# Four blocks of two transformer layers in split fp32: both activation buffers start at another byte of 128

## The chip, the cores and the metric

The kernel runs on one core of a Trainium2 chip. The metric is the time of one execution in microseconds of the device, as the median of several runs. Engines in the profile: PE is TensorE's matmuls, PEld its weight loads, DVE VectorE, ACT ScalarE, POOL GpSimd, SP the engine that issues most transfers.

## What is computed

A sequence of 256 tokens of width 1024 goes through two models of two layers each. Each layer has two FFNs with SwiGLU and hidden width 2816, and between them a mixer: two banded attentions and a stick-breaking one in the first model, with cross-attention to a memory of 256 rows, and differential attention beside an mLSTM in the second. All of it is fp32. The greater part of the arithmetic is matrix products of this kind:

```python
def swiglu(h, w_gu, w_down):
    g, u = jnp.split(h @ w_gu, 2, axis=-1)
    return (jax.nn.silu(g) * u) @ w_down
...
x = x + FFN_SCALE * rmsnorm(swiglu(h, ffn1_w_gu[l], ffn1_w_down[l]), ffn1_norm_post[l])
h = rmsnorm(x, mix_norm_pre[l])
z = h @ w_in[l]
```

## The kernel before

Activations lie transposed: the 1024 features are 8 chunks (`C`) of 128 partitions, the 256 tokens (`T`) the free dimension. The weights come as a stream of 829 tiles of 128 x 1024 fp32 (512 KB), in the order in which they are used. SP loads tile n into one of four slots of `raw`. ScalarE rounds it to the type float32r into `w_hi` (line 1037), VectorE writes the rest `raw - w_hi`, rounded too, into `w_lo` (line 1471); both are rings of six slots. An activation is split in the same way into a high and a low part. A product is then three matmuls in float32r: high weight by high activation, high weight by low activation, low weight by high activation. TensorE issues nearly all of its matmuls through one helper, `mm`, at line 457.

The split activations live in two buffers, `a` and `b`, of shape 128 x 8 x 2 x 256: for each chunk the 256 columns of the high part and behind them the 256 of the low part. There are four forms in which TensorE reads them:

- `w_tile`, `three` and `tail_part`: per chunk three matmuls, each with 128 x 128 of weights stationary and 256 columns of `a` or `b` moving; 24 matmuls for one weight tile.
- `pair_tile` and `first_three`: as high and low part lie side by side, `w_hi` takes both in one matmul of 512 columns (`both`), and `w_lo` the high part in one of 256; eight chunks, 16 matmuls. This is used for gate and up of the FFNs.
- `down` in `ffn`: the hidden values of one step are in a chunk of the other buffer, and 24 matmuls of 256 columns add the product to the accumulators.
- `v_half`: the values of attention, with the roles exchanged: 128 columns of `a` or `b` stationary and 256 columns of a weight tile moving.

`a` is written by the norm ahead of each stage (`high` at line 1057 on ScalarE, `low` at line 1498 on VectorE), `b` by the hidden values in the FFN (lines 1092 and 1471) and by the outputs of attention. After a cross-attention the two exchange their roles, which is why both appear in both in the profile. TensorE takes the tiles in the order of the stream and waits per tile for the splits, and per chunk for the norm when the activation is fresh.

The order of the allocations is `raw`, a gap of 16 bytes, `a`, `b`, a gap of 48 bytes, `x`, `z` and the other buffers, a gap of 48 bytes, `w_hi`, `w_lo`, constants. Each allocation takes a multiple of 32 bytes. In the program's table of addresses, per partition, `raw` starts at byte 16512, `a` at 32928, `b` at 49312, `x` at 65760, `z` at 73952 and `w_hi` at 163168. Modulo 128 that is 0 for `raw`, 32 for `a` and `b`, and 96 for `x`, `z`, `w_hi` and `w_lo`. All pieces of `a`, `b` and the weight tiles that a matmul takes begin at multiples of 512 bytes from the start of their buffer, so these remainders are the remainders of every matmul's operands.

Of the kernel before, what the change touches and what calls it, by code (L numbers as in the profile page):

```python
# [24 lines left out]
F32R = mybir.dt.float32r  # L25
# [4 lines left out]
P = 128  # L30
D = 1024
T = 256
C = D // P
# [108 lines left out]
def build(nc, stream_d, x_d, mem_d, vec_d, con_d, biasa_d, biasc_d, heads_d, out_d, stages=STAGES):  # L142
    total = sum(TILES[s] for s, _ in stages)
    with ExitStack() as ctx:
        def sb(name, shape, dt=F32):
            return ctx.enter_context(nc.sbuf_tensor(name, shape, dt))
# [3 lines left out]

        raw = sb("raw", [P, RAW, D])
        sb("gap_a", [P, 4])
        a_two, b_two = sb("a", [P, C, 2, T], F32R), sb("b", [P, C, 2, T], F32R)
        a_hi, a_lo = a_two[:, :, 0, :], a_two[:, :, 1, :]
        b_hi, b_lo = b_two[:, :, 0, :], b_two[:, :, 1, :]
        sb("gap_x", [P, 12])
# [2121 lines left out]
```

## Time and profile before

| | us |
|---|---|
| median of 3 runs | 2693.83 (2691.82 to 2696.59) |
| the profiled execution | 2694.12 |
| its span in the trace | 2692.0 |
| PE busy | 2613.1 (97%) |
| PEld busy | 2410.1 (90%) |
| DVE busy | 1920.5 (71%) |
| ACT busy | 1502.9 (56%) |

A row of a group has the line, engine and operation, then output <- inputs by the buffers' names, for a matmul the moving operand first and the stationary one second, then shapes and count; behind the bar the busy time of the group, the mean of one instruction in ns, the idle time of the engine just before them and who ended it. A matmul's duration is modelled and holds its way through the array, so that durations of successive ones overlap; how often TensorE starts one is read from the starts in the timeline. The timeline merges neighbours of the same kind (x2). "Clock" (PEclk) is the share of TensorE's full clock that was granted.

### The profile page before, as it was taken

Reading aid. Unit: us, or ns where it says so; the run is one execution under the profiler, and the core shown is the slowest. Engines: PE = TensorE matmul, PEld = TensorE weight load, DVE = VectorE, ACT = ScalarE, POOL = GpSimd, SP = SyncE. Lnnn points to the kernel's source line nnn. Section 1 sums busy time; section 2 is a strip of 40 time slices with the busy share of each in tenths; the row PEclk is TensorE's granted clock in tenths of the full one; section 3 lists DMA queues with packets and bytes.
Section 4 is the critical chain, followed back from the end, with each engine's and each line's share of the span. In section 5 each row is a group of like instructions: output and inputs, shape, how many; then the busy total and the mean of one; then the engine's idle time right before and its main releaser. Section 6 shows DMA issues by size and latency. Waiting matters only on the chain.

```text
span 2692.0 us, 51716 instructions
## 1 busy us (share of the span) xinstructions
PE 2613.1 (97%) x18604; PEld 2410.1 (90%) x18604; DVE 1920.5 (71%) x3131; ACT 1502.9 (56%) x2579; POOL 201.6 (7%) x280
## 2 busy tenths in 40 slices
PE   8999799999999999999999999999999999999998
PEld 7998699999998899999998998989989999988997
DVE  7777676778777576777777667777787776676876
ACT  6556556556555656556555555655565555555554
POOL 0001001000000201000000160000000005300000
PEclk9999899999999999999999999999999999999999
DMA  7554244655554344555654543545545545335553
GB/s 261 202 189 135 87 134 156 225 202 183 186 187 157 102 158 136 188 186 169 204 187 142 179 157 103 165 154 185 186 154 187 187 143 171 126 118 165 172 187 109
DMA packets 122821, 445.80 MB, mean 166 GB/s; under 512 B 13688, under 2 KB 14712, under 8 KB 122688
## 3 DMA queue, kind: packets, MB, share of 16 engines
q1 hardware_dynamic: 120816, 436.79, 49.0%
q0 software_dynamic: 1872, 7.17, 0.7%
q8 instruction: 92, 1.51, 0.2%
q14 instruction: 41, 0.34, 0.0%
HBM read 442.86 MB, written 1.05 MB: 165 GB/s over the span
## 4 chain that ended last, share of the span: by engine, by line
PE 92%; DVE 5%; ACT 2%; issue 1%; DMA 0%; SPq 0%; ACTq 0%; DVEq 0%
PE bank L457 91%; DVE w_lo L1471 1%; PE bank L808 1%; DVE rt L1699 1%; DVE z L1537 1%; ACT w_hi L1037 0%; DVE rt L1493 0%; DVE x L1530 0%; DVE a L1498 0%; ACT score L1271 0%; DMA x<-in_x_dram 0%; DVE rstd_x L1490 0%; DMA raw<-in_stream_dram 0%; ACT L1245 0%; DVE z L1643 0%
## 5 line engine op out<-in xcount | busy, mean ns | idle before, releaser
L457 PE MATMUL bank<-a,w_hi 128*128 128x256 f32 (+1 forms) x5360 | 1342.3, 329 | 38.5 <-DVE a L1498 38.0
L1471 DVE TENSOR_TENSOR w_lo<-raw,w_hi 128x1024 fp32r<-128x1024 f32 x829 | 1016.7, 1230 | 278.3 <-ACT w_hi L1037 277.1
L457 PE MATMUL bank<-a,w_lo 128*128 128x256 f32 x3736 | 1013.2, 282 | 0.0
L457 PEld LDWEIGHTS bank<-a,w_hi 128*128 128x128 f32 x5360 | 897.4, 190 | 126.2 <-issue 45.7
L1037 ACT CAST w_hi<-raw 128x1024 fp32r<-128x1024 f32 x829 | 858.0, 1046 | 42.6 <-DMA raw<-in_stream_dram 35.4
L457 PE MATMUL bank<-b,w_hi 128*128 128x256 f32 (+1 forms) x4096 | 859.5, 301 | 3.6 <-DVE b L1498 2.6
L457 PEld LDWEIGHTS bank<-a,w_lo 128*128 128x128 f32 x3736 | 709.2, 190 | 16.8
L457 PEld LDWEIGHTS bank<-b,w_hi 128*128 128x128 f32 x4096 | 656.9, 188 | 40.6 <-issue 3.5
L457 PE MATMUL bank<-b,w_lo 128*128 128x256 f32 x2400 | 658.6, 280 | 0.0
L457 PEld LDWEIGHTS bank<-b,w_lo 128*128 128x128 f32 x2400 | 450.4, 188 | 5.6
L1084 ACT COPY pt<-bank 128x256 f32<-128x256 f32 x176 | 65.5, 372 | 219.1 <-PE bank L457 219.1
L1080 ACT COPY pt<-bank 128x256 f32<-128x256 f32 x176 | 65.3, 371 | 219.2 <-PE bank L457 219.2
L2033 POOL TENSOR_TENSOR score<-score 128x256 f32<-128x256 f32 x45 | 38.2, 848 | 1367.6 <-ACT score L1067 1366.6
L1550 DVE TENSOR_TENSOR sil<-bank,pt 128x256 f32<-128x256 f32 x176 | 74.6, 424 | 88.6 <-ACT pt L1080 88.6
L1092 ACT CAST b<-hmid 128x256 fp32r<-128x256 f32 x132 | 53.7, 407 | 142.6 <-PE bank L457 133.1
L457 PE MATMUL bank<-w_hi,a 128*128 128x256 f32 x736 | 129.6, 280 | 0.0
L457 PEld LDWEIGHTS bank<-w_hi,a 128*128 128x128 f32 x736 | 111.7, 188 | 3.4 <-issue 2.9
L1643 DVE TENSOR_TENSOR z<-bank,rstd_x 128x256 f32<-128x256 f32 x125 | 52.8, 422 | 83.3 <-PE bank L457 83.1
L1556 DVE TENSOR_TENSOR hmid<-bank,pt 128x256 f32<-128x256 f32 x176 | 74.5, 424 | 44.2 <-ACT pt L1084 44.1
L457 PE MATMUL bank<-w_lo,a 128*128 128x256 f32 x368 | 102.3, 278 | 0.0
L1471 DVE TENSOR_TENSOR b<-hmid,b 128x256 fp32r<-128x256 f32 x132 | 56.0, 424 | 45.7 <-ACT b L1092 45.7
L1088 ACT ACTIVATE sil<-sil 128x256 f32<-128x256 f32 x176 | 74.3, 422 | 21.3 <-DVE sil L1561 21.2
(185 smaller groups left out, 2130.7 us busy)
## 6 DMA issues: line engine op xcount, KB each, us to landing
raw<-in_stream_dram SPq DMA_DIRECT2D x829, 512.0 KB, 3.3
z<-in_biasc_dram POOLq DMA_DIRECT2D x6, 512.0 KB, 4.5
z<-in_biasa_dram POOLq DMA_DIRECT2D x3, 512.0 KB, 4.4
x<-in_x_dram SPq DMA_DIRECT2D x2, 512.0 KB, 8.0
v<-in_mem_dram POOLq DMA_DIRECT2D x2, 512.0 KB, 6.3
out_dram<-x SPq DMA_DIRECT2D x8, 128.0 KB, 1.9
con<-in_con_dram POOLq DMA_DIRECT2D x1, 912.0 KB, 6.6
vec<-in_vec_dram POOLq DMA_DIRECT2D x1, 417.0 KB, 5.6
```

Source lines behind the costliest of these rows:

```text
L457: return nc.tensor.matmul(out, lhsT, rhs, start=start, stop=stop, skip_group_check=shared)
L808: last = nc.tensor.transpose(out[:, col:col + P], p[:, src:src + P], ident)
L1037: nc.scalar.copy(w_hi[:, slot, :], raw[:, raw_slot, :]).then_inc(hi_split, 1)
L1080: nc.scalar.copy(pt[:, j % 2, 0:T], bank[ffn_banks(j, after_mixer)[0]][:, T:2 * T]).then_inc(gate_rest, 1)
L1084: nc.scalar.copy(pt[:, j % 2, T:2 * T], bank[ffn_banks(j, after_mixer)[1]][:, T:2 * T]).then_inc(up_rest, 1)
L1088: nc.scalar.activation(sil[:, jj, :], sil[:, jj, :], ACT.Silu).then_inc(silu_done, 1)
L1092: nc.scalar.copy(high_of["b"][:, jj, :], hmid[:, jj, :]).then_inc(hhi_done, 1)
L1471: return nc.vector.tensor_tensor(out, a, hi.bitcast(F32), ALU.subtract)
L1550: nc.vector.tensor_tensor(sil[:, jj, :], bank[ffn_banks(j, after_mixer)[0]][:, 0:T], pt[:, jj, 0:T], ALU.add)\
L1556: nc.vector.tensor_tensor(hmid[:, jj, :], bank[ffn_banks(j, after_mixer)[1]][:, 0:T], pt[:, jj, T:2 * T], ALU.add).then_inc(up_read, 1)
L1643: nc.vector.tensor_tensor(z[:, tile, :], out[:, 0:T], rstd[norm][:, :], ALU.mult).then_inc(w_evac, 1)
L2033: ins = nc.gpsimd.tensor_tensor(sq[:, 0, :], sq[:, 0, :], sq[:, c, :], ALU.add)
```

## The change

Both buffers get a room that is 32 words (128 bytes) longer than their content. The content of `a` begins 2 words (8 bytes) into its room, that of `b` 30 words (120 bytes) into its own. Modulo 128, `a` goes from 32 to 40 and `b` from 32 to 24. Everything allocated behind them moves up by 256 bytes and keeps its remainder modulo 128; `raw` stays. The views `a_hi`, `a_lo`, `b_hi`, `b_lo` are taken as before, and no instruction, order or wait is touched.

```diff
-        a_two, b_two = sb("a", [P, C, 2, T], F32R), sb("b", [P, C, 2, T], F32R)
+        ROOM, A_AT, B_AT = 32, 2, 30
+        a_room, b_room = sb("a", [P, C * 2 * T + ROOM], F32R), sb("b", [P, C * 2 * T + ROOM], F32R)
+        a_two, b_two = (room[:, at:at + C * 2 * T].rearrange("p (c s t) -> p c s t", s=2, t=T)
+                        for room, at in ((a_room, A_AT), (b_room, B_AT)))
         a_hi, a_lo = a_two[:, :, 0, :], a_two[:, :, 1, :]
         b_hi, b_lo = b_two[:, :, 0, :], b_two[:, :, 1, :]
```

## Rows read from the trace of the kernel before

**Rows 1.** Page: busy time of each engine; the chain by engine; PEclk in 40 slices

```profile
PE 2613.1 (97%) x18604; PEld 2410.1 (90%) x18604; DVE 1920.5 (71%) x3131; ACT 1502.9 (56%) x2579; POOL 201.6 (7%) x280
...
PEclk9999899999999999999999999999999999999999
...
PE 92%; DVE 5%; ACT 2%; issue 1%; DMA 0%; SPq 0%; ACTq 0%; DVEq 0%
```

**Rows 2.** Chain of waits in order of time: start us, us, what

```profile
423.43 440.26 PE bank L457 x3024
```

**Rows 3.** Matmul groups by line and shape: names, shapes, count, busy us, mean ns, idle

```profile
L457 PE MATMUL bank<-a,w_lo 128*128 128x256 f32 x3736 | 1013.2, 282 | 0.0
...
L457 PE MATMUL bank<-a,w_hi 128*128 128x512 f32 x2112 | 751.4, 398 | 25.7 <-DVE a L1498 25.7
...
L457 PE MATMUL bank<-b,w_lo 128*128 128x256 f32 x2400 | 658.6, 280 | 0.0
...
L457 PE MATMUL bank<-b,w_hi 128*128 128x256 f32 x3392 | 612.1, 281 | 3.6 <-DVE b L1498 2.6 <-DVE b L1471 1.0
L457 PE MATMUL bank<-a,w_hi 128*128 128x256 f32 x3248 | 590.9, 284 | 12.8 <-DVE a L1498 12.3 <-DVE w_lo L1471 0.5
...
L457 PE MATMUL bank<-b,w_hi 128*128 128x512 f32 x704 | 247.4, 395 | 0.0
L457 PE MATMUL bank<-w_hi,a 128*128 128x256 f32 x736 | 129.6, 280 | 0.0
...
L457 PE MATMUL bank<-w_hi,b 128*128 128x256 f32 x256 | 48.5, 292 | 0.0
```

**Rows 4.** Timeline, quick stretch: start us, us, engine, line, tiles, shape, count

```profile
309.02 0.39 PE L457 MATMUL bank<-b,w_hi 128*128 128x256 f32 x2
...
310.72 0.39 PE L457 MATMUL bank<-b,w_hi 128*128 128x256 f32 x2
```

**Rows 5.** Timeline, the stretch after it

```profile
339.15 0.40 PE L457 MATMUL bank<-a,w_hi 128*128 128x256 f32 x2
...
342.68 0.40 PE L457 MATMUL bank<-a,w_hi 128*128 128x256 f32 x2
```

**Rows 6.** Timeline, two pair tiles of an FFN, their first row and the next tile's

```profile
1108.22 0.39 PE L457 MATMUL bank<-a,w_hi 128*128 128x512 f32 x1
...
1113.83 0.40 PE L457 MATMUL bank<-b,w_hi 128*128 128x256 f32 x2
```

**Rows 7.** Timeline, ordinary fp32 matmuls and the start after them

```profile
1004.02 1.89 PE L457 MATMUL bank<-z 128*128 128x256 f32 x8
1005.55 0.58 PE L457 MATMUL bank<-a,w_hi 128*128 128x256 f32 x2
```

**Rows 8.** Timeline, weight tiles moving: a quick stretch, then a usual one

```profile
1509.35 0.39 PE L457 MATMUL bank<-w_hi,a 128*128 128x256 f32 x2
...
1511.05 0.39 PE L457 MATMUL bank<-w_hi,a 128*128 128x256 f32 x2
...
1564.19 0.40 PE L457 MATMUL bank<-w_hi,a 128*128 128x256 f32 x2
...
1567.38 0.40 PE L457 MATMUL bank<-w_hi,a 128*128 128x256 f32 x2
```

**Rows 9.** Groups on VectorE and ScalarE that write weights, a and b; one wait

```profile
L1471 DVE TENSOR_TENSOR w_lo<-raw,w_hi 128x1024 fp32r<-128x1024 f32 x829 | 1016.7, 1230 | 278.3 <-ACT w_hi L1037 277.1
...
L1037 ACT CAST w_hi<-raw 128x1024 fp32r<-128x1024 f32 x829 | 858.0, 1046 | 42.6 <-DMA raw<-in_stream_dram 35.4 <-PE bank L457 5.6 <-DVE z L1643 0.7
...
L1471 DVE TENSOR_TENSOR b<-hmid,b 128x256 fp32r<-128x256 f32 x132 | 56.0, 424 | 45.7 <-ACT b L1092 45.7
...
L1498 DVE SCALAR_TENSOR_TENSOR a<-x,vec,a 128x256 fp32r<-128x256 f32 x80 | 43.5, 551 | 2.8 <-ACT a L1057 2.8
...
L1057 ACT ACTIVATE a<-x,vec 128x256 fp32r<-128x256 f32 x80 | 39.8, 506 | 44.8 <-DVE x L1530 30.3 <-DVE x L1519 12.8 <-DMA x<-in_x_dram 1.3
...
PE bank L457 <- DVE a L1498: 38.0, 8, 11.1
```

## Prediction

> **What bounds the kernel now.** I read the page first, then the groups by line and shape, then the timeline of TensorE in a few stretches, start against start. The page says TensorE: its matmul side is busy 2613.1 us of 2692.0 us, and the chain that ended last runs 92% over it [rows 1]. The DMA queue, VectorE and ScalarE stand beside it: VectorE has 1920.5 us of work, ScalarE 1502.9 us. In the chain by time there are single pieces such as 440.26 us with 3024 matmuls of the one line that issues nearly all of them, in which nothing but TensorE stands [rows 2]. So the question is what one matmul costs, and a change in the addresses of its moving operand can only pay there.
>
> What is issued: 14,264 matmuls of 256 columns in the rounded fp32 type and 2,816 of 512 columns [rows 3] (of the tiles with weights moving the rows show the ones with `w_hi`; for two of these there is one with `w_lo`); of the first, 1,488 have a weight tile moving and `a` or `b` stationary, 12,776 have `a` or `b` moving. The durations in these rows are modelled and overlap, so I take starts. In a stretch of the even mixer's output tiles 15 matmuls take 1.70 us from the first row to the last, 113.3 ns each [rows 4]. A few microseconds later, after four matmuls of sums of squares, the same tile form takes 3.53 us for 30, 117.7 ns each [rows 5]; over all such stretches I find 117.8. [...] Both paces stay unchanged for dozens of matmuls and go over from one tile to the next; they change only where something else comes in between. The clock is granted at nine tenths or more in nearly every slice of the span [rows 1]. The pairs of FFN tiles (one of 512, one of 256 with the same moving data) take 5.61 us for 16 pairs, 350.6 ns each, 350.3 over the whole trace, where three matmuls at the quick pace would be 340.0 [rows 6]. [...] Counting runs of six starts over the whole timeline, about 900 of 8,300 matmuls with `a` or `b` moving are at the quick pace (11%), and about 750 of 1,300 with a weight tile moving (58%); the latter have a quick and a usual state too, 113.3 ns (15 in 1.70 us) and 117.8 ns (27 in 3.18 us) [rows 8].
>
> **The change, part by part.** It adds no instruction and no wait and removes none. (1) `a` starts 8 bytes later, `b` 8 bytes earlier than before modulo 128: the program's table of addresses has both at 32 modulo 128, `raw` at 0, `w_hi`, `w_lo`, `x` and `z` at 96. Afterwards `a` is at 40, `b` at 24. (2) Everything behind `b` moves by 256 bytes, which leaves its remainder modulo 128 and 256; `raw` and the weight ring move apart by those 256 bytes. (3) 256 bytes of memory more are used.
>
> (2) and (3) I cost at nothing. The splits of a tile take ScalarE 1046 ns and VectorE 1230 ns [rows 9], 829 times, 858 and 1017 us of 2692, and are covered by the three or so matmul tiles (24 x 0.118 = 2.8 us each) that TensorE has in hand. If that cover were gone, a tenth more on VectorE's split would cost 829 x 0.12 = 102 us; but the remainders of all its three operands stay, and TensorE waits only 0.5 us in all for it by name in the rows of 256 columns [rows 3].
>
> (1) also touches ScalarE and VectorE where they write `a` and `b`: the 176 splits of the FFN's hidden values, 424 ns each on VectorE (132 of them into `b`), and 112 norm tiles of 505 to 551 ns [rows 9]. TensorE waits for the norm tiles at the start of a stage, 38.0 us in all for `a`, eight waits [rows 9]. If each of the eight tiles of a stage took 10% more, 14 stages would lose 14 x 8 x 0.05 = 6 us at most, since they overlap; I see no cause and take 0, with -1 and +6 as ends.
>
> What is left is the pace of 17,080 matmuls. No row of before has a moving operand of this type at another remainder than 32 or 96, so I bound it from both sides. The good end: all matmuls reach the quick state. Some 9,960 x 0.89 = 8,900 with `a` or `b` moving outside of the pairs (12,776 less 2,816) and 620 with weights moving, times 4.45 ns, are 42 us; 2,816 pairs times 10.3 ns are 29 us; together 71 us, 2623 us. [...] The slope between 512 and 256 columns [rows 6] is (350.3 - 2 x 117.8) = 114.7 ns for 256 columns, 0.45 ns a column, so four columns are 1.8 ns, and 17,080 x 1.8 = 31 us. Together with the 6 us above, 2694 + 44 = 2738 us.
>
> Between these ends I choose by the nearest row. The state depends on how the stream of weights, read for the next matmul, lies in time and address against the moving stream; `a` and `w` are now 64 bytes apart modulo 128, whichever of them moves. [...] I think it likelier than not that another distance lets more stretches fall into the quick state, because at present so few do: 11% leaves much to win and little to lose. I take the share that the tiles with weights moving already have, 58%: (0.58 - 0.11) x 9,960 x 4.45 ns = 20.8 us; pairs unchanged. The sum is 2694.12 (the profiled execution, 2692.0 of span and 2.1 around it) - 20.8 + 0 = 2673 us; the median of the runs shown is 0.3 us below that execution, so 2673 stands for the median too.
>
> [...]
>
> **The rivals.** *Quicker* (0.43): the case above, 2673 us; its own range goes from 2625 to 2688. For it: two states for one and the same instruction at one remainder, and the poor share of the better. Against it: nothing in before shows that the remainder sets the share.
>
> *Nothing happens* (0.25): the two states are set by the order of instructions and the moment at which a stretch starts, not by the address. For it: `a` at 32 moving and weights at 96 moving have the same two paces to 0.1 ns; the 2694 us that result are today's. Against it: that pair is mirror symmetric, 64 bytes both ways.
>
> *Slower* (0.32): the reads of the moving operand no longer start on a whole 16-byte piece, and one piece more is fetched per matmul. [...]
>
> That the change doesn't do what it says can be left out: the allocation rounds to 32 bytes, the room of 128 is a multiple of it, and the offsets lie inside the room.
>
> **How the numbers follow.** Forecast 2673 us. Quicker and slower are both open, so the range goes from 2635 (three quarters of the way from 2673 to the good end) to 2720 (slower, half hidden, and a little more); I put one in ten outside at each end. A measurement can tell about 0.2%, 5.4 us: faster is the first case nearly whole with none of the second, 0.43; same 0.25; slower 0.32.
>
> **What would show it.** In the trace after: the starts of matmuls in the even mixer's output, the FFN down tiles and the long projections of the mixers; I expect steps of 113.3 ns in more of them and no third pace. If slower, the steps themselves would be longer by 1 to 2 ns in every state, and 512 columns by the same absolute amount. VectorE's splits into `a` and `b` should keep 424 ns. I am wrong if the starts show the same states at the same places, if a third pace appears, or if `a` and `b`, shifted in opposite senses, go opposite ways and cancel. It would also be wrong if the pairs move: they are a third of the time, and I have left them at 350.3 ns.

## The result, and the profile after

| | before | after |
|---|---|---|
| median of the runs side by side, us | 2695.21 | 2730.32 |
| lowest to highest, us | 2691.82 to 2697.19 | 2727.91 to 2731.82 |
| span of the profiled execution, us | 2692.0 | 2727.7 |
| matmul side of TensorE busy, us | 2613.1 | 2650.6 |

The ratio is 1.0131 with an interval of 1.0113 to 1.0148: the changed kernel is slower by 35 us. The forecast was 2673 us with a range of 2635 to 2720, so it had the sign wrong, and the time lies outside the range, though inside the outer bounds of 2623 and 2738.

The page of the kernel after, with its span, the busy times, the granted clock in 40 slices and the chain by engine, answers to [rows 1]:

```profile
span 2727.7 us, 51716 instructions
...
PE 2650.6 (97%) x18604; PEld 2449.1 (90%) x18604; DVE 1921.2 (70%) x3131; ACT 1503.1 (55%) x2579; POOL 200.8 (7%) x280
...
PEclk9999899999999999999999999999999999999999
...
PE 94%; DVE 4%; ACT 1%; issue 0%; DMA 0%; SPq 0%; DVEq 0%; ACTq 0%
```

The counts of instructions are those of before, the slices of the clock are the same digit by digit, and the granted clock has the same mean in both, 0.987. VectorE and ScalarE have the same work to 1 us. Only TensorE has more: 37.5 us on its matmul side, which covers the 35.7 us by which the span grew.

The groups of the kernel after by line and shape (count, then busy us and mean ns, then idle time before them). The change inserts three lines, so line 457 of before is 460 here. The rows answer to [rows 3] and [rows 9]:

```profile
L460 PE MATMUL bank<-a,w_lo 128*128 128x256 f32 x3736 | 1024.7, 285 | 0.0
...
L460 PE MATMUL bank<-a,w_hi 128*128 128x512 f32 x2112 | 755.5, 399 | 25.2 <-DVE a L1501 25.1
...
L460 PE MATMUL bank<-b,w_hi 128*128 128x256 f32 x3392 | 622.7, 283 | 3.5 <-DVE b L1501 2.5 <-DVE b L1474 1.0
L460 PE MATMUL bank<-a,w_hi 128*128 128x256 f32 x3248 | 607.0, 287 | 12.8 <-DVE a L1501 12.1 <-DVE w_lo L1474 0.6
...
L460 PE MATMUL bank<-w_hi,a 128*128 128x256 f32 x736 | 133.2, 284 | 0.0
...
L1474 DVE TENSOR_TENSOR w_lo<-raw,w_hi 128x1024 fp32r<-128x1024 f32 x829 | 1016.0, 1230 | 281.7 <-ACT w_hi L1040 281.2
...
L1474 DVE TENSOR_TENSOR b<-hmid,b 128x256 fp32r<-128x256 f32 x132 | 56.0, 425 | 50.5 <-ACT b L1095 50.5
...
L1501 DVE SCALAR_TENSOR_TENSOR a<-x,vec,a 128x256 fp32r<-128x256 f32 x80 | 43.6, 552 | 2.6 <-ACT a L1060 2.6
```

Every matmul group of `a` and `b` with 256 columns has grown by 1 to 4 ns a matmul, also those with a weight tile moving (280 to 284). Those that write `a` and `b` take what they took: 425 ns against 424, 552 against 551. The idle times that end with the norm tiles are a little shorter. So the time is in the pace of the matmuls alone.

The timeline of TensorE in the kernel after (start us, us, engine, line, tiles, shape, count): first the even mixer's output tiles, the stage of [rows 4]; then a down tile of an FFN that reads `a`; then two pair tiles, the place of [rows 6]:

```profile
317.10 0.40 PE L460 MATMUL bank<-b,w_hi 128*128 128x256 f32 x2
...
319.26 0.40 PE L460 MATMUL bank<-b,w_hi 128*128 128x256 f32 x2
...
600.92 0.40 PE L460 MATMUL bank<-a,w_hi 128*128 128x256 f32 x2
...
603.85 0.40 PE L460 MATMUL bank<-b,w_hi 128*128 128x512 f32 x1
...
1113.49 0.40 PE L460 MATMUL bank<-a,w_hi 128*128 128x512 f32 x1
...
1119.15 0.40 PE L460 MATMUL bank<-b,w_hi 128*128 128x256 f32 x2
```

18 matmuls on `b` in 2.16 us are 120.0 ns each, 24 on `a` in 2.93 us are 122.1, 16 pairs in 5.66 us are 353.8. A third pace has appeared, and the quick one of 113.3 ns is gone: among all runs of six starts in a row with `a` or `b` moving and 256 columns there were 900 matmuls at 113.3 ns before, and none is left.

To see where the 35.7 us went I add up, over the whole timeline, the distance from each start to the next, by what moves and what is stationary. Distances over 300 ns are kept apart as stalls, and everything that isn't one of these matmuls is "other". The same sums are given for the experiments below that need them:

```
us, start to start        before  after   zero  aonly  bonly both16   all8   half rest208 minus4  plus4 split124 joint32
a moving, 256              583.6  600.9  583.4  602.2  584.1  590.6  604.6  569.2   567.5  587.3  592.9    581.7   570.7
a moving, pairs            733.7  740.9  738.5  740.8  738.4  736.8  739.5  738.0   735.7  722.7  752.7    719.7   737.0
b moving, 256              599.2  610.0  583.8  587.1  610.2  606.8  612.4  583.8   580.7  599.2  621.3    594.8   583.5
b moving, pairs            246.2  244.7  247.3  247.3  246.1  246.7  247.7  247.3   246.4  241.8  250.8    247.6   247.3
weights moving, a and b    175.3  179.6  175.6  178.9  175.9  178.8  181.5  177.1   182.4  180.1  179.4    177.0   177.8
other                      287.6  289.9  287.3  289.2  288.9  287.7  289.7  289.3   290.1  289.1  287.7    287.8   289.8
stalls                      44.3   39.9   41.6   43.4   41.3   41.4   40.3   42.4    44.3   41.9   40.5     42.4    45.8
```

From before to after: `a` with 256 columns +17.3, `b` +10.8, pairs on `a` +7.2 and on `b` -1.5, weights moving +4.3, other +2.3, stalls -4.4; together 36.0 us. The mean pace of the runs of six is 121.0 ns on `a` and 119.6 on `b`, where it was 117.8 and 117.9 in the usual state of before.

### The profile page after: what moved, and what is told of

Its sections match the earlier page's. It is cut to its first block, busy times and chain, and to the rows that moved or that the text cites. A ratio compares the mean times of both kernels' runs of the same rounds, so it can differ in the third digit from the quotient of the medians.

```text
span 2727.7 us, 51716 instructions
## 1 busy us (share of the span) xinstructions
PE 2650.6 (97%) x18604; PEld 2449.1 (90%) x18604; DVE 1921.2 (70%) x3131; ACT 1503.1 (55%) x2579; POOL 200.8 (7%) x280
## 4 chain that ended last, share of the span: by engine, by line
PE 94%; DVE 4%; ACT 1%; issue 0%; DMA 0%; SPq 0%; DVEq 0%; ACTq 0%
PE bank L460 93%; PE bank L811 1%; DVE rt L1702 1%; DVE z L1540 0%; DVE w_lo L1474 0%; DVE rt L1496 0%; DVE x L1533 0%; DVE a L1501 0%; DMA x<-in_x_dram 0%; ACT w_hi L1040 0%; ACT score L1274 0%; ACT L1248 0%; DVE z L1830 0%; DVE z L1708 0%; DVE z L1833 0%
## 5 line engine op out<-in xcount | busy, mean ns | idle before, releaser
L460 PE MATMUL bank<-a,w_hi 128*128 128x256 f32 (+1 forms) x5360 | 1362.4, 331 | 37.9 <-DVE a L1501 37.2
L460 PE MATMUL bank<-a,w_lo 128*128 128x256 f32 x3736 | 1024.7, 285 | 0.0
L460 PEld LDWEIGHTS bank<-a,w_hi 128*128 128x128 f32 x5360 | 907.9, 192 | 125.6 <-issue 45.0
L460 PE MATMUL bank<-b,w_hi 128*128 128x256 f32 (+1 forms) x4096 | 868.8, 302 | 3.5 <-DVE b L1501 2.5
L460 PEld LDWEIGHTS bank<-a,w_lo 128*128 128x128 f32 x3736 | 716.8, 192 | 16.6
L1559 DVE TENSOR_TENSOR hmid<-bank,pt 128x256 f32<-128x256 f32 x176 | 74.4, 423 | 45.7 <-ACT pt L1087 45.5
```

What stands on the lines that cost most here:

```text
L460: return nc.tensor.matmul(out, lhsT, rhs, start=start, stop=stop, skip_group_check=shared)
L1559: nc.vector.tensor_tensor(hmid[:, jj, :], bank[ffn_banks(j, after_mixer)[1]][:, 0:T], pt[:, jj, T:2 * T], ALU.add).then_inc(up_read, 1)
```

## The experiments

The theory with which I went on, *place*: TensorE's pace depends on where its two operands lie, with several fixed paces, and the change moved both to bad places. The rival, *piece*, is an assumption for which no trace has a row: an operand that doesn't start on a multiple of 16 bytes costs one fetch more. In question was also whether the 128 bytes of room count for something, although I had costed them at nothing. The line numbers and edits are against the kernel after. The kernel before was measured beside each group of runs; its median lay between 2694.6 and 2696.7 us, so that times of different groups compare to some 2 us.

**zero: the rooms alone.** The buffers start where their rooms start; everything behind still lies 256 bytes later.

```diff
-        ROOM, A_AT, B_AT = 32, 2, 30
+        ROOM, A_AT, B_AT = 32, 0, 0
```

> Both rooms kept, but a and b start at the beginning of them: remainder 32 as before, everything behind them 256 bytes further on. If the remainders of a and b carry the loss: the time of before, 2695 us within 5, with quick stretches of 113.3 ns again. If the 256 bytes between raw and the weight ring, or a larger period than 128, carry it: about 2730 us and no quick stretch.

Measured: 2684.86 us, ratio 0.9963 (0.9951 to 0.9976). It is faster than before, so the rooms alone aren't neutral. The page and two groups of zero:

```profile
PE 2600.9 (97%) x18604; PEld 2395.8 (89%) x18604; DVE 1920.2 (72%) x3131; ACT 1503.2 (56%) x2579; POOL 201.2 (8%) x280
...
L460 PE MATMUL bank<-b,w_hi 128*128 128x256 f32 x3392 | 597.4, 279 | 3.6 <-DVE b L1501 2.6 <-DVE b L1474 1.0
L460 PE MATMUL bank<-a,w_hi 128*128 128x256 f32 x3248 | 590.3, 283 | 13.0 <-DVE a L1501 12.7 <-DVE w_lo L1474 0.3
```

The gain is in `b` (281 to 279 ns; 15.4 us by the sums), where 2,442 matmuls now run at 113.3 ns instead of 258; `a` is as before. Here is what I had overlooked. In the table of addresses `a` and `b` both lay at 160 modulo 256 before. The room of `a` pushes `b` by 128 bytes, not by 256: in zero `a` is still at 160, but `b` at 32. Modulo 128 both numbers are 32, and that was the only remainder that I had followed for `b`. Against zero, the right control, the two shifts of 8 bytes cost 2730.3 - 2684.9 = 45 us, not 35.

**aonly and bonly: one shift each.**

```diff
-        ROOM, A_AT, B_AT = 32, 2, 30
+        ROOM, A_AT, B_AT = 32, 2, 0        (aonly)
+        ROOM, A_AT, B_AT = 32, 0, 30       (bonly)
```

> a 8 bytes on (40 modulo 128), b at the start of its room (32), all else as in the kernel with both at 32 that took 2685 us. If each buffer pays for itself, in proportion to its matmuls: a has 9,100 of the matmuls that read a or b as moving data, b 6,500, so the 45 us between 2685 and 2730 split into 26 for a: 2711 us. Quick stretches of 113.3 ns on b only.

> b 8 bytes below (24 modulo 128), a at 32. By the same division 19 us for b: 2704 us; and as b held most of the quick stretches of the 2685 us kernel (2442 matmuls against 558), it may well be the larger part, 2710 us. Opposite senses that cancel would show here as one of the two being faster than 2685 us: I don't expect it.

Measured: aonly 2709.07 us, 1.005 (1.0033 to 1.0067); bonly 2708.05 us, 1.0051 (1.0034 to 1.0068). Over zero that is 24.2 and 23.2 us, together 47.4 where both at once gave 45.5. The two shifts add up; 8 bytes upward and 8 bytes downward (120 upward) both cost, and nothing cancels. By the sums each one's cost sits in its own buffer: +18.8 us on `a` and +3.3 on `b` in aonly, 0.7 and +26.4 in bonly.

**both16: both at 16 bytes into their rooms**, a multiple of 16, so that *piece* has nothing to charge.

```diff
-        ROOM, A_AT, B_AT = 32, 2, 30
+        ROOM, A_AT, B_AT = 32, 4, 4
```

> a and b both 16 bytes further, at 48 modulo 128. Theory of the piece (a moving operand that doesn't start on a multiple of 16 bytes costs one piece more): 2695 us within 5. Rival, the distance between moving operand and weights modulo 128 (64 before, 56 and 72 after, 48 here): another time than before by at least 10 us, on a side that the theory doesn't give.

Measured: 2712.82 us, 1.006 (1.0043 to 1.0077), 28 us over zero. A start on 16 bytes doesn't bring the time back. The paces are 118.9 ns on `a` and 119.0 on `b`, without a quick stretch. *Piece* had 2695 us here and is 18 us off.

**all8: the distance kept modulo 128.** `a`, `b` and both weight rings are shifted by 8 bytes, so moving and stationary operand stand to each other as in zero, as far as remainders modulo 128 go. Modulo 256 this holds for `w_hi` (at 104) and not for `w_lo`: the room of `w_hi` is 128 bytes longer, so `w_lo` lies at 232, where zero has it at 96.

```diff
-        ROOM, A_AT, B_AT = 32, 2, 30
+        ROOM, A_AT, B_AT = 32, 2, 2
...
-        w_hi = sb("w_hi", [P, RING, D], F32R)
-        w_lo = sb("w_lo", [P, RING, D], F32R)
+        W_AT = 2
+        w_hi, w_lo = (sb(name, [P, RING * D + 32], F32R)[:, W_AT:W_AT + RING * D].rearrange("p (r d) -> p r d", d=D)
+                      for name in ("w_hi", "w_lo"))
```

> a, b, w_hi and w_lo all 8 bytes further, at 40, 40, 104 and 104 modulo 128: the distances are those of before, but no operand starts on a multiple of 16 bytes. Theory of the piece: at least the loss of the change, 2730 us or more (the weights pay too). Distance: 2695 us within 5, with the quick stretches back.

Measured: 2739.19 us, 1.0164 (1.0147 to 1.0181), the slowest until then. The distance modulo 128 alone isn't it, and *piece*, which had 2730 us or more, is not refuted here. As a third of the matmuls take `w_lo`, at another distance modulo 256, this run doesn't show by itself that 8 bytes cost at an unchanged distance; the next experiment does. Now the weight tiles as the moving operand are also slower (+5.9 us over zero).

**table: the disputed cost by itself.** Nothing but matmuls of the kernel's forms, on data that never changes, with the moving operand at 16 remainders modulo 128 in steps of 8 bytes and the weights at four.

> This kernel computes nothing of the reference; it copies x and runs on TensorE alone, with nothing else at work, the three forms of the kernel (three matmuls of 256 columns, a pair of 512 and 256, roles exchanged) for 16 remainders of the moving operand (0 to 120 in steps of 8) against weights at 96, 104, 112 and 64. Theory of the piece: two levels, even rows (multiples of 16) at 113 to 118 ns, odd rows 1 to 2 ns higher, the same for all four weight positions. Distance: a curve with period 128 that moves along by 8, 16 and -32 bytes with the weights. If the two paces of before are made by the other engines' accesses, one pace alone for all.

Each place has its own pace, and it repeats. With weights at 96 modulo 128 and the moving operand at 32 (modulo 256: 224 and 160), both paces of [rows 4, 5] come out, 113.3 ns behind one kind of lead-in and 117.8 behind another, with every other engine idle: the two states belong to TensorE alone, not to traffic of others. The other 15 remainders gave 116.7 to 122.3 ns. With weights at 104 and the moving operand at 40, the same distance with both 8 bytes off a multiple of 16, it is 120.8 and 120.9: 8 bytes on both sides cost, with the distance kept modulo 256 as well. Even multiples of 8 averaged 117 to 118, odd ones 119.5 to 121 ns, for all four places of the weights; that is what *piece* had forecast for the averages, though not the spread inside each kind. It explains the direction of after, but not zero, which this table can't tell from before.

**table_two: modulo 256**, 32 offsets in steps of 8 bytes, weights at 96, 224 and 352 modulo 512, each behind three lead-ins.

> Nothing of the reference is computed; TensorE alone, one moving buffer of the kernel's own layout at 32 offsets (0 to 248 bytes in steps of 8, its room at 0 modulo 256) against weights at 96, 224 and 352 modulo 512. Theory of the piece: offsets that are 8 modulo 16 average 1.7 ns above the others for every position of the weights. Period 128: offset r and r + 128 give the same pace, and so do weights at 96 and 224. Period 256: they don't, but 96 and 352 agree.

The timeline of TensorE in table_two (`x` is the ordinary fp32 matmul that marks the change from one stretch to the next, `m` the moving operand), for offsets 32, 152, 168 and 208 with weights at 96, in this order:

```profile
95.60 6.00 PE L53 MATMUL bank<-m,w 128*128 128x256 f32 x48
101.53 1.13 PE L53 MATMUL bank<-x 64*128 64x256 f32 x4
102.59 5.72 PE L53 MATMUL bank<-m,w 128*128 128x256 f32 x48
108.14 1.03 PE L53 MATMUL bank<-x 128*128 128x256 f32 x4
...
396.13 6.11 PE L53 MATMUL bank<-m,w 128*128 128x256 f32 x48
402.17 1.13 PE L53 MATMUL bank<-x 64*128 64x256 f32 x4
...
435.90 6.21 PE L53 MATMUL bank<-m,w 128*128 128x256 f32 x48
442.04 0.70 PE L53 MATMUL bank<-x 64*128 64x256 f32 x2
...
536.80 5.82 PE L53 MATMUL bank<-m,w 128*128 128x256 f32 x48
542.55 1.13 PE L53 MATMUL bank<-x 64*128 64x256 f32 x4
543.61 5.76 PE L53 MATMUL bank<-m,w 128*128 128x256 f32 x48
549.21 1.03 PE L53 MATMUL bank<-x 128*128 128x256 f32 x4
```

48 matmuls and the way into the next mark take 5.93 us at offset 32, 6.04 at 152 (`b` of after), 6.14 at 168 (`a` of after) and 5.75 at 208, all behind the same lead-in. The step into the mark is the same in all, so the differences count: 6.04 - 5.93 is 2.3 ns a matmul, 6.14 - 5.93 is 4.4, and 5.75 - 5.93 is -3.8. Behind the other lead-in (a mark of 64 rows before, one of 128 rows after) offset 208 takes 5.60, 0.15 less, but offset 32 takes 5.55, 0.38 less: there the same 48 instructions on the same data have gone over to the quick pace. (In table, at the same two places, the quick pace came behind the mark of 128 rows and the usual one behind that of 64: it isn't the form of the mark by itself.) From the starts inside the stretches:

```
moving at (mod 256), weights at 96     lead-in 1   lead-in 2   pairs (per 256 columns)
 32 and 160  (b of zero; a of before)     117.8       113.3       117.8 / 117.6
168          (a of after)                 122.3       119.9       118.0
152          (b of after)                 119.9       120.0       115.4
208                                       113.3       113.3       117.8
```

The weights at 96 and 352 gave the same table row by row, while rows of one table that are 128 apart differ: what counts is the place modulo 256. The table for 224 is that for 96 moved by 128 in 21 of the 32 rows to half a nanosecond; in the others at least one lead-in shows another pace. And two lead-ins don't show all paces of a place: in table_four, where other offsets run ahead, 168 took 120.2 ns behind both. With `a` at 168 and `b` at 152 this is the result after: about 121 and 120 ns and no quick state, the pairs on `b` a little better.

**half: both at 32 modulo 256** instead of both at 160, with no shift inside a room. The gap ahead of `a` is 128 bytes longer, and `b` keeps a room of 128 bytes more behind it, so that everything behind lies where it lies after the change.

```diff
-        sb("gap_a", [P, 4])
-        ROOM, A_AT, B_AT = 32, 2, 30
-        a_room, b_room = sb("a", [P, C * 2 * T + ROOM], F32R), sb("b", [P, C * 2 * T + ROOM], F32R)
+        sb("gap_a", [P, 36])
+        A_AT, B_AT = 0, 0
+        a_room, b_room = sb("a", [P, C * 2 * T + 0], F32R), sb("b", [P, C * 2 * T + 32], F32R)
```

> No room at a, but a gap of 128 bytes more ahead of it; a and b both at 32 modulo 256, where b alone was in the 2685 us kernel (before: 160 modulo 256 for both), weights at 96 modulo 256 as in all. If a period of 256 bytes decides which locked pace a stretch gets, a now gets b's share of quick stretches: about half of some 3,600 matmuls at 117.8 ns go to 113.3, 8 us or more, so 2677 us or less. If only the 256 bytes that the weight ring moves made the gain of 10 us: 2685 us.

Measured: 2672.79 us, 0.9924 (0.9907 to 0.994). It beats both kernels. TensorE's timeline in half, a stage on `a` that stays quick for 60 matmuls (6.80 us, 113.3 ns each) where [rows 5] has the usual pace:

```profile
337.64 0.39 PE L460 MATMUL bank<-a,w_hi 128*128 128x256 f32 x2
...
344.44 0.39 PE L460 MATMUL bank<-a,w_hi 128*128 128x256 f32 x2
```

By the sums `a` at 32 instead of 160 is worth 14.4 us and `b` 15.4. Yet the microkernels gave the offsets 32 and 160 the same two paces. So the place sets which paces there are, and what comes before a stretch in the kernel sets which of them it falls into.

The traces show where 32 is luckier than 160. In the FFNs 120 stretches of a down tile (a few of two) read `b` right behind a pair tile on `a`, and 40 read `a` right behind a pair tile on `b`. At 113.3 ns are:

```
down tiles quick            before   zero  aonly  bonly   half  joint32  split124
on b, behind a pair on a   0 of 120    114    120      0    120      120         0
on a, behind a pair on b    0 of 40      0      0      0     40       40         0
```

Of the 29.8 us that half gains over before on 256 columns, these 160 stretches (4,224 matmuls x 4.5 ns) are 19. No table has a pair tile as its lead-in.

**rest208: both at 208 modulo 256**, where the table has the quick pace behind both lead-ins.

```diff
-        sb("gap_a", [P, 4])
-        ROOM, A_AT, B_AT = 32, 2, 30
-        a_room, b_room = sb("a", [P, C * 2 * T + ROOM], F32R), sb("b", [P, C * 2 * T + ROOM], F32R)
+        sb("gap_a", [P, 16])
+        A_AT, B_AT = 4, 36
+        a_room, b_room = sb("a", [P, C * 2 * T + 32], F32R), sb("b", [P, C * 2 * T + 64], F32R)
...
-        sb("gap_x", [P, 12])
+        sb("gap_x", [P, 36])
```

> a and b both at 208 modulo 256 (80 modulo 128), by a gap and rooms; weights at 96 modulo 256 as before, everything behind b 512 bytes on. In the table for TensorE alone this row had 113.3 ns after both lead-ins, where 32 and 160 had it after one, and 117.8 ns a 256 columns in pairs (117.6 at 160, 117.8 at 32). If the table holds in the kernel: nearly all tiles of 256 columns with a or b moving at 113.3, 9,960 at most 4.45 ns less than the 117.2 to 120.2 ns of before, pairs as slow as with 32; about 2660 us, below the 2673 of both at 32. If the pace in the kernel comes from the other engines' accesses as well: no better than 2673 us.

Measured: 2671.76 us, 0.9914 (0.9897 to 0.9931), where 2660 was expected. The tiles of 256 columns did mostly what the table said (3,528 matmuls on `a` and 3,768 on `b` at 113.3 ns, of some 8,200 that stand in runs of six), but the matmuls with weights moving, which I had left where they were, cost 7 us more, and the pairs 2 us more than in before. A gain of one form is partly paid by another.

**table_three: which relation.** 16 moving offsets against 8 places of the weights in steps of 16 bytes, and the exchanged roles.

> Nothing of the reference is computed. TensorE alone, moving operand at 16 offsets modulo 256 (steps of 16 bytes) against 8 positions of the weights (0 to 112), three forms and the exchanged roles. If only the distance between the two streams modulo 256 counted, the diagonals of the table would be constant; the tables so far say they are not (quick at 208 against 96, but at 144 against 104 and 176 against 240), so I expect one to three quick cells (113.3 ns) in each column and no diagonal.

I had not expected a diagonal, and there is one, for steps of 32 bytes. Paces behind the two lead-ins:

```
moving - weights = 112:  (144,32) 113.3/113.3  (176,64) 113.3/113.3  (208,96) 113.3/113.3
                         (128,16) 120.0/120.0  (160,48) 120.0/120.0  (192,80) 120.0/120.0
moving - weights = -64:  (32,96)  117.7/113.3  (0,64)   117.8/113.3  (224,32) 113.3/117.8
                         (16,80)  113.3/113.3  (48,112) 113.3/113.3  (208,16) 113.3/113.3
```

Within a line both addresses move by 32 together and the paces stay (at (224,32) the two lead-ins have swapped them); from the upper line of each pair to the lower one they move by 16, and the paces change. These are chosen cells. Over the whole table, of the 95 cells that have a partner 32 bytes on for both operands 80 have the same two paces within 0.7 ns (in whatever order of the lead-ins); of the 111 with a partner 16 bytes on, 16 have. So the table is in the main one of the distance modulo 256 and of the place of the weights modulo 32.

**joint32: this relation in the whole kernel.** half, with everything behind `raw` moved by 32 bytes more: `a` and `b` at 64, the weights at 128.

```diff
-        sb("gap_a", [P, 4])
-        ROOM, A_AT, B_AT = 32, 2, 30
-        a_room, b_room = sb("a", [P, C * 2 * T + ROOM], F32R), sb("b", [P, C * 2 * T + ROOM], F32R)
+        sb("gap_a", [P, 44])
+        A_AT, B_AT = 0, 0
+        a_room, b_room = sb("a", [P, C * 2 * T + 0], F32R), sb("b", [P, C * 2 * T + 32], F32R)
```

> The kernel of 2673 us with everything behind raw 32 bytes further on: a and b at 64, weights at 128 modulo 256, the distance as before. If the distance modulo 256 decides for remainders of the weights that are equal modulo 32, as the diagonals of the third table say: 2673 us within 5. If each operand's own remainder counts, or the distance to raw on the splitting engines: another time, 2690 us or more.

Measured: 2672.73 us, 0.9909 (0.9892 to 0.9925), half's time to 0.1 us, and half's sums for each form of matmul within 1.5 us (the stalls differ by 3.4). The relation holds in the kernel for this one step; the step of 16 bytes, which should change the time, was not tried there.

**table_four: steps of 4 bytes**, 64 offsets with weights at 96, to put *piece* to a test of its own: 1024 bytes that begin 4, 8 or 12 bytes off a multiple of 16 all lie in 65 pieces of 16.

> Nothing of the reference is computed. TensorE alone, 64 offsets of the moving operand in steps of 4 bytes, weights at 96. Theory of the piece of 16 bytes: offsets that are 4, 8 and 12 modulo 16 average alike, 1.7 to 2.5 ns above 0 modulo 16. [...] Nothing but the start within 32 or 64 bytes: the four classes modulo 16 don't differ.

Averages over 16 offsets of a class, ns per 256 columns:

```
offset mod 16    lead-in 1   lead-in 2   pairs
      0             118.3       117.4    117.2
      4             121.4       121.5    118.7
      8             119.8       120.2    118.0
     12             118.3       118.4    115.4
```

12 costs about what 0 costs (1 ns more behind the second lead-in), and less in the pairs. A charge for the 65th piece can't give that.

**minus4 and plus4: the same in the kernel.** Both buffers 124 or 4 bytes above the room's start; 12 and 4 modulo 16. Modulo 256, plus4 has `a` at 164 and `b` at 36, 4 above their places in zero. In minus4 the two are exchanged: `a` is at 28, 4 below 32, and `b` at 156, 4 below 160.

```diff
-        ROOM, A_AT, B_AT = 32, 2, 30
-        a_room, b_room = sb("a", [P, C * 2 * T + ROOM], F32R), sb("b", [P, C * 2 * T + ROOM], F32R)
+        A_AT, B_AT = 31, 31        (minus4)
+        a_room, b_room = sb("a", [P, C * 2 * T + 32], F32R), sb("b", [P, C * 2 * T + 32], F32R)
```

```diff
-        ROOM, A_AT, B_AT = 32, 2, 30
+        ROOM, A_AT, B_AT = 32, 1, 1        (plus4)
```

> a and b 4 bytes below a remainder of 32 modulo 128 (28 and 156 modulo 256), all else as in the kernel of 2685 us. Theory of the piece: the moving data lie in one piece of 16 bytes more, about 2730 us again. Table: 118.4 and 117.7 ns in tiles of 256 (6 and 16 us more), 114.9 and 114.4 in pairs instead of 117.5 (23 us less): 2685 us within 8.

> a and b 4 bytes on from the kernel of 2685 us (36 modulo 128; 164 and 36 modulo 256). Theory of the piece: like 8 bytes on for both, about 2730 us. Table: 122.2 and 121.7 ns in tiles of 256 where the kernel has 117.2 and 114.6, 119.9 and 118.9 in pairs where it has 117.5: 24 + 36 + 18 us more and a few for the exchanged roles, about 2765 us.

Measured: minus4 2684.44 us, 0.9951 (0.9934 to 0.9968); plus4 2749.59 us, 1.0194 (1.0177 to 1.0211). Two shifts by 4 bytes, both with the 65th piece, are 65 us apart. The control of minus4 would be a kernel with `a` at 32 and `b` at 160, which no run has. By the sums of half (`a`) and before (`b`) I estimate it at 1168.4 us for 256 columns and 984.2 for the pairs; zero has 1167.2 and 985.8, so zero can stand for it. Against that minus4 costs nothing: `a` with 256 columns has lost quick stretches (587.3 against 569.2 us at 32), `b` is where it was at 160 (599.2), and the pairs have gained some 20 us, where the 65th piece should have cost them too. *Piece* has fallen. TensorE's timeline, two pair tiles and a down tile on `b`: first minus4, in the next fence plus4:

```profile
1114.72 0.39 PE L460 MATMUL bank<-a,w_hi 128*128 128x512 f32 x1
...
1120.23 0.40 PE L460 MATMUL bank<-b,w_hi 128*128 128x256 f32 x2
```

```profile
1109.49 0.40 PE L460 MATMUL bank<-a,w_hi 128*128 128x512 f32 x1
...
1115.23 0.41 PE L460 MATMUL bank<-b,w_hi 128*128 128x256 f32 x2
...
1118.16 0.40 PE L460 MATMUL bank<-a,w_hi 128*128 128x512 f32 x1
```

The 16 pairs take 5.51 us in minus4 (344.4 ns each) and 5.74 in plus4 (358.8), where before had 5.61 [rows 6]. The down tile of plus4 has 24 matmuls in 2.93 us, 122.1 ns each.

**split124: the best place of each.** `a` at 124 modulo 256, best for pairs in table_four, `b` at 32.

```diff
-        sb("gap_a", [P, 4])
-        ROOM, A_AT, B_AT = 32, 2, 30
-        a_room, b_room = sb("a", [P, C * 2 * T + ROOM], F32R), sb("b", [P, C * 2 * T + ROOM], F32R)
+        sb("gap_a", [P, 56])
+        A_AT, B_AT = 7, 40
+        a_room, b_room = sb("a", [P, C * 2 * T + 8], F32R), sb("b", [P, C * 2 * T + 64], F32R)
...
-        sb("gap_x", [P, 12])
+        sb("gap_x", [P, 24])
```

> a at 124 modulo 256, 4 bytes below a multiple of 16, because a has three quarters of the pair tiles and that row of the table had 114.4 ns in pairs and 117.0 in tiles of 256; b at 32 as in the kernel of 2673 us. By the table 20 us less in a's pairs, 11 more in its other tiles: 2664 us. If the table can't be carried over, 2673 or above.

Measured: 2677.0 us, 0.9927 (0.991 to 0.9944), where 2664 was expected. Against half the pairs on `a` gave 18.3 us as forecast, `a` with 256 columns took back 12.5, and then, not foreseen, `b` 11.0, although neither it nor the weights had moved modulo 256. The group of `b` in split124:

```profile
L460 PE MATMUL bank<-b,w_hi 128*128 128x256 f32 x3392 | 608.2, 282 | 3.8 <-DVE b L1501 2.7 <-DVE b L1474 1.0
```

282 ns against 279 in zero at the same place. Of some 4,100 matmuls on `b` 906 were quick, not 2,508. Which ones were lost can be read from the traces. A down tile on `b` behind a pair tile on `a`, up to the next pair tile, first in half, then in split124:

```profile
1108.80 0.40 PE L460 MATMUL bank<-b,w_hi 128*128 128x256 f32 x2
...
1111.53 0.39 PE L460 MATMUL bank<-a,w_hi 128*128 128x512 f32 x1
```

```profile
1108.57 0.40 PE L460 MATMUL bank<-b,w_hi 128*128 128x256 f32 x2
...
1111.39 0.39 PE L460 MATMUL bank<-a,w_hi 128*128 128x512 f32 x1
```

24 matmuls take 2.73 us in half and 2.82 in split124. It is so for all of them: 120 of 120 such tiles are quick in half and none in split124, while of the 40 or so stretches on `b` behind other work 20 are quick in half and 19 in split124. `a` is the only operand that moved modulo 256, so the pace on `b` hangs on the place of the tile on `a` that runs ahead of it. The pace of a tile can't be read from its own place alone.

## Why the prediction was wrong

1. *What bounds the kernel: right.* The 36 us are in the matmuls of one line; VectorE's and ScalarE's splits kept their times, and the waits for the norm tiles didn't grow, so the term of -1 to +6 us for them was 0.
2. *The step that failed: "another distance lets more stretches fall into the quick state, because at present so few do".* I read the 11% as room for a gain, and took the share of the matmuls with weights moving as the measure, for -20.8 us. That term measured +28.1 us. The trace had shown that there were two paces at one place. It had not shown how many paces other places have, and nothing in it said that the quick one must exist there. In the runs a place has its own set: 113.3 and 117.8 at 32 or 160, 119.9 and 122.3 at 168, about 120 at 152. After the change no stretch on `a` or `b` was quick. Of the 28.1 us on 256 columns, about 15 on `a` (4,854 x 3.2 ns) and 9 on `b` (5,063 x 1.7 ns) are the new paces over the usual one, and 900 x 4.5 ns = 4 us are the quick matmuls lost. I had named a third pace as a sign that I would be wrong, and had put no price on it. The matmuls with weights moving had no term either and took 4.3 us more: 720 of 1,290 in runs of six were quick before and none after, although the weight tiles, their moving operand, had kept their place; with `a` alone shifted 18 were left, with `b` alone 588.
3. *The rooms, costed at nothing.* Term (2), what lies behind `b`, "leaves its remainder modulo 128 and 256": that is true, and by the sums of zero the weights moving cost 0.3 us more. What is missing stands in (1), which gives the shift of `b` modulo 128 only: the room of `a` pushes `b` by 128 bytes before its own offset. This has a price: zero, which has the rooms alone, is 0.4% (some 10 us) faster than before. The change is thus the sum of a gain of 10 us from the rooms and a cost of 45 us from the offsets. Any estimate by remainders modulo 128 was blind to the first.
4. *The pairs, left at 350.3 ns:* they are at 353.7 on `a` and 348.2 on `b` in after, start to start, +7.2 and -1.5 us by the sums. Of the +7.2, 4.8 are in zero already, where neither `a` nor the weights have changed modulo 256; after split124 I'd put it down to what runs ahead, but no run shows that for the pairs.
5. *Slower:* in full 2694 + 31 + 7 = 2732 us, nearest in the number and wrong in the mechanism. It charged 1.8 ns, four columns of 0.45 ns, to each of 17,080 matmuls for a 65th piece of 16 bytes, which 1024 bytes touch when they begin 8 bytes off a multiple of 16 (1,488 of them have a weight tile moving, whose start stays on a multiple of 16, so by its own account it was 28 us and not 31). That the operand is read in such pieces was my assumption, and so was that half of the charge might be hidden; no run shows either. So no run shows the 31 us in the bound of 2738 (2694 + 31 + 7 for the quick state lost, 1,650 x 4.45 ns, + 6 for the norm tiles), nor the 15 us in the range's upper end (2694 + 15 + 7 = 2716 and a little more). What they show is that minus4, with a 65th piece by that count, costs nothing over zero, and plus4, with one too, costs 65 us; the pairs on `b` got faster in after. Had I believed in it, minus4 would have been forecast at 2730 and come out at 2684. A number that fits is no proof of its cause.
6. *The cancelling of `a` and `b`* did not take place: 24.2 + 23.2 us alone, 45.5 together.
7. *The chances:* faster had 0.43 and slower 0.32 on a term for which the trace held no row. With only the rows at hand, two paces of which most matmuls had the worse, a shift could as well lead to worse sets. The range ended at "half hidden" on the bad side, while the full rival comes to 2732 and the bound to 2738; it should have reached there.

What stays open is the physical cause: why the distance modulo 256 and the weights' place modulo 32 go with the pace (80 of 95 entries of table_three), and what a pair tile at one place leaves behind that one at another place doesn't. The runs show the relation, with exceptions in the tables, and not the reason.

## What to carry to other kernels

When a kernel is bound by float32r matmuls, read their pace from start to start, not from modelled durations (in after 283 to 287 ns for 256 columns with `w_hi`, where the starts were about 120 to 121 apart), and look for several fixed paces at one form. In these runs they went with the places of moving and stationary operand modulo 256 (113.3 to 122.3 ns with weights at 96 in table_two), so any change in the allocations, a few "harmless" bytes of padding included, can also change the pace: compare it with a control that moves the same addresses and does nothing else. Find the place with a small table of matmuls alone, then try it in the whole kernel, because what runs ahead decides which pace is taken; here 128 bytes more ahead of `a` and 128 behind `b` (half) were worth 0.8%, and the best table entry (rest208) no more than that.

## What the runs showed of the hardware

- One and the same float32r matmul on the same addresses has two paces, at the places of before 113.3 and 117.8 ns for 256 columns, and keeps one through a whole stretch (48 matmuls at offset 32 in table_two) with every other engine idle. The ordinary fp32 matmuls of 256 columns start 215.9 ns apart (in before, seven steps from 1004.016 to 1005.527 us, the place of [rows 7]).
- Over the addresses the pace goes from 113.3 to 122.3 ns in steps of 8 bytes, to 123.5 in one entry of table_three and to 124.5 in table_four (offset 228), and repeats modulo 256. The same step of 32 bytes on both operands leaves it in 80 of 95 entries, 16 bytes on both in 16 of 111.
- The pace of a stretch hangs on what ran ahead of it: with `b` and the weights at the same places, 120 of 120 down tiles on `b` behind pair tiles on `a` took 113.3 ns with `a` at 32 and none with `a` at 124.
- By the moving operand's start modulo 16, 4 is the dearest (121.4 ns on average), then 8 (about 120), and 12 is about as cheap as 0 (118.3), and in the pairs the cheapest of all (115.4 per 256 columns). In the whole kernel both buffers 4 bytes above and both 4 bytes below a place that is 32 modulo 128 are 65 us apart, 2.4%.
